# A hybrid attention and mixture-of-experts layer: the ring of expert weights refills four couples' places instead of three

## The reference

```python
def per_sequence(args):
    hs, cs = args
    a = jnp.einsum('sd,edf->sef', hs, w_gate)      # w_gate, w_up: (32, 1024, 256)
    u = jnp.einsum('sd,edf->sef', hs, w_up)
    act = jax.nn.silu(a) * u * cs[..., None].astype(hs.dtype)
    return jnp.einsum('sef,efd->sd', act, w_down)  # w_down: (32, 256, 1024)
x = x + hierarchical_moe(...)
return rms_norm(x, norm_final_g)
```

## Time and profile before

| | |
|---|---|
| median of 3 runs | 372.0 us (370.66, 372.0, 376.49) |
| the profiled execution's own time | 372.67 us |
| its span, first to last instruction | 370.9 us |
| granted TensorE clock, mean | 0.96 of full speed |
| TensorE busy | 311.2 us (84%) |
| VectorE, ScalarE, GpSimd busy | 167.8, 117.9, 42.2 us |
| moved by the DMA engines | 121.68 MB, mean 328 GB/s |
| VectorE's first copy of the end (line 1387) | starts at 362.66 us |

### The profile page before, as it was taken

One profiled execution on the slowest core, in us unless ns is written; L12 is line 12 of the kernel. 1 busy time (PEld: TensorE's weight loads), 2 busy tenths in 40 slices (PEclk: granted clock), 3 DMA queues, 4 the chain that ended last, 5 costly groups with the idle time before them and its releaser, 6 DMA issues.

```text
span 370.9 us, 11439 instructions
## 1 busy us (share of the span) xinstructions
PE 311.2 (84%) x4700; PEld 240.6 (65%) x4701; DVE 167.8 (45%) x445; ACT 117.9 (32%) x275; POOL 42.2 (11%) x65
## 2 busy tenths in 40 slices
PE   1799999999999899549979897979998997586571
PEld 1699989799775445237767665657766765566350
DVE  2637354565164514874435444344444443231334
ACT  4736156463244215621212222222222221120222
POOL 1200001451404023820000000000000000000002
PEclk9999999999999999968999999999999999588996
DMA  8999892080839782985999969999999999999953
GB/s 253 360 386 387 289 418 122 2 341 11 330 139 422 203 350 97 338 342 217 413 421 414 415 264 418 421 412 422 416 414 421 412 424 420 412 423 414 417 232 113
DMA packets 31434, 121.68 MB, mean 328 GB/s; under 512 B 5432, under 2 KB 7760, under 8 KB 23216
## 3 DMA queue, kind: packets, MB, share of 16 engines
q1 hardware_dynamic: 31264, 121.15, 82.8%
q10 hardware_dynamic: 144, 0.15, 0.1%
HBM read 120.24 MB, written 1.05 MB: 327 GB/s over the span
## 4 chain that ended last, share of the span: by engine, by line
PE 60%; DMA 7%; issue 7%; DVE 7%; SPq 7%; ACT 5%; DVEq 5%; POOL 0%; POOLq 0%; ACTq 0%
PE bank L448 12%; PE bank L717 8%; PE bank L513 8%; PE bank L659 7%; DMA ring<-in_w_up_dram 6%; PE bank L442 6%; SPq L328 4%; PE bank L696 4%; PE bank L669 4%; SPq L335 2%; ACT yb L960 2%; PE bank L462 2%; DVEq L1369 2%; PE bank L706 2%; DVEq L1368 2%
## 5 line engine op out<-in xcount | busy, mean ns | idle before, releaser
L696 PEld LDWEIGHTS bank<-ring,hT 128*32 128x32 f32 x2176 | 64.9, 118 | 33.3 <-issue 32.0
L696 PE MATMUL bank<-ring,hT 128*32 128x128 f32 x2176 | 70.4, 291 | 18.3 <-DMA ring<-in_w_up_dram 9.0
L1364 DVE SCALAR_TENSOR_TENSOR yb<-bank,pp,yb 64x512 fp32r<-64x512 f32 x36 | 27.0, 749 | 45.2 <-ACT yb L960 44.6
L659 PE MATMUL bank<-pp,qk 128*128 128x64 bf16 x912 | 31.7, 197 | 11.5 <-DVE pp L1297 8.6
L1107 DVE TENSOR_TENSOR unit_lo<-ring,unit_hi 128x2048 fp32r<-128x2048 f32 (+1 forms) x12 | 26.3, 2205 | 32.1 <-ACT unit_hi L783 32.0
L659 PEld LDWEIGHTS bank<-pp,qk 128*128 128x128 bf16 x912 | 29.2, 100 | 16.3 <-DVE pp L1297 11.6
L960 ACT ACTIVATE yb<-bank,pp 64x512 fp32r<-64x512 f32 x36 | 24.6, 682 | 29.0 <-PE bank L717 28.5
L717 PE MATMUL bank<-ring,pp 128*32 128x512 f32 x272 | 32.7, 598 | 0.1
L1022 POOL TENSOR_TENSOR stats<-stats 128x1 f32<-128x1 f32 (+1 forms) x7 | 4.3, 620 | 228.9 <-DVE stats L1395 205.3
L513 PE MATMUL bank<-ring,qk 128*128 128x512 f32 x64 | 29.3, 598 | 0.0
L950 ACT ACTIVATE pp<-bank 128x128 f32<-128x128 f32 x18 | 5.0, 277 | 70.8 <-PE bank L696 70.8
(11 more groups left out here) (195 smaller groups left out, 439.7 us busy)
## 6 DMA issues: line engine op xcount, KB each, us to landing
ring<-in_w_gate_dram SPq DMA_DIRECT2D x30, 1024.0 KB, 12.6
ring<-in_w_up_dram SPq DMA_DIRECT2D x30, 1024.0 KB, 16.0
ring<-in_w_down_dram SPq DMA_DIRECT2D x30, 1024.0 KB, 15.8
ring<-in_w_in_dram SPq DMA_DIRECT2D x5, 2048.0 KB, 20.3
ring<-in_w_out_dram SPq DMA_DIRECT2D x1, 4096.0 KB, 12.9
ring<-in_w_in_dram SPq DMA_DIRECT2D x2, 1024.0 KB, 7.7
work<-in_x_dram SPq DMA_DIRECT2D x2, 512.0 KB, 4.6
spare<-in_w_gate_dram SPq DMA_DIRECT2D x1, 1024.0 KB, 15.9
```

The lines of the kernel that those rows point to most:

```text
L659: last = mm(p_hg[:, k * CP:(k + 1) * CP], hs[:, i, t, k, :], selb[:, t, :], start=(t == 0 and i == 0), stop=(t == NT - 1 and i == 2))
L696: last = mm(p_gu[b:b + CAP, w * P:(w + 1) * P], hg[:, k, CAP * e:CAP * (e + 1)], w_gu[at[e]][:, w, k, h, :], start=(k == 0), stop=(k == KD ...
L1364: V.scalar_tensor_tensor(out=yb[half][rest, :], in0=p_y[rows, :], scalar=wcol[rows, :], in1=yb[half][rows, :].bitcast(fp32), op0=ALU.mult, ...
```

## The change

The ring goes round all four couples' places: places 6 and 7 are refilled too, and couple q from 4 on goes into the places of couple q - 4. TensorE's loop has four bodies and goes three times round; SyncE's loop over refills likewise has four and goes twice round, behind four refills written out. The last norm's weights no longer lie in `work`, which now holds the weights of couple 15, but in the head of the ring's place 0, which couple 12 used last; SyncE waits for couple 12's gate products before it issues them. The transfers themselves, their order and their sizes stay.

```diff
-TURN = 3
+RINGED = 6
+TURN = 4
-FIRST = TURN + 1
-LOOPS = (COUPLES - FIRST) // TURN
+LOOPS = COUPLES // TURN - 1
...
-        ring = sb("ring", [P, 2 * TURN * EXPERT])
+        ring = sb("ring", [P, RINGED * EXPERT])
...
-        gfin = work[:, 0:D]
+        gfin = ring[:, 0:D]
...
         def places(q):
-            if q == TURN:
-                return EXTRA, EXTRA + 1
-            s = q if q < TURN else (q - FIRST) % TURN
-            return 2 * s, 2 * s + 1
+            return 2 * (q % TURN), 2 * (q % TURN) + 1
...
             for q in range(TURN):
-                refill(q, [(2 * (q + FIRST) + i, places(q + FIRST)[i]) for i in range(2)])
+                refill(q, [(2 * (q + TURN) + i, places(q)[i]) for i in range(2)])
             with sp.Fori(1, LOOPS) as g:
                 for j in range(TURN):
-                    refill(g * TURN + (FIRST - TURN + j), [(2 * (g * TURN + (FIRST + j)) + i, places(FIRST + j)[i]) for i in range(2)])
+                    refill(g * TURN + j, [(2 * (g * TURN + (TURN + j)) + i, places(j)[i]) for i in range(2)])
+
+            sp.wait_ge(gate_done, sp.value_load(base[0:1, COUPLES - TURN + 1:COUPLES - TURN + 2], min_val=1, max_val=ITEMS_MAX))
             sp.dma_start(gfin, I["norm_final_g"].rearrange("(o d) -> o d", o=1).to_broadcast([P, D])).then_inc(gfin_in, 16)
...
             for q in range(TURN):
                 couple(q, places(q), (1, 1))
-            couple(TURN, places(TURN), (1, 1))
             with pe.Fori(0, LOOPS) as g:
                 for j in range(TURN):
-                    couple(g * TURN + (FIRST + j), places(FIRST + j), (g + 2, g + 2))
+                    couple(g * TURN + (TURN + j), places(j), (g + 2, g + 2))
```

More of the change, by code:

```diff
@@ L49 @@
 PASSES_MAX = SEQ // CAP
-TURN = 3
+RINGED = 6
+TURN = 4
 EXPERT = 3 * KD * FE
-FIRST = TURN + 1
-LOOPS = (COUPLES - FIRST) // TURN
-assert FIRST + LOOPS * TURN == COUPLES
+LOOPS = COUPLES // TURN - 1
+assert (LOOPS + 1) * TURN == COUPLES
 ITEMS_MAX = COUPLES * PASSES_MAX
@@ L216, in layer_program @@
         wcol = pp[:, M0 + 960:M0 + 961]
-        place = [ring[:, s * EXPERT:(s + 1) * EXPERT] for s in range(2 * TURN)] + [work[:, :]]
-        EXTRA = 2 * TURN
+        place = [ring[:, s * EXPERT:(s + 1) * EXPERT] for s in range(RINGED)] + [work[:, :]]
         gu_at = [s[:, 0:2 * KD * FE] for s in place] + [spare[:, :]]
@@ L245, in layer_program @@
         blk_in = [sem(f"blk_in{b}") for b in range(6)]
-        gate_in = [sem(f"gate_in{p}") for p in range(EXTRA + 2)]
-        up_in = [sem(f"up_in{p}") for p in range(EXTRA + 2)]
-        dn_in = [sem(f"dn_in{p}") for p in range(EXTRA + 2)]
+        gate_in = [sem(f"gate_in{p}") for p in range(2 * TURN)]
+        up_in = [sem(f"up_in{p}") for p in range(2 * TURN)]
+        dn_in = [sem(f"dn_in{p}") for p in range(2 * TURN)]
         out_done = sem("out_done")
@@ L339, in load @@
                 load_dn(e, e)
-            load_gu(2 * TURN + 1, EXTRA + 1)
+            load_gu(RINGED + 1, RINGED + 1)
             sp.wait_ge(w_lo_ready, 10)
@@ L368, in _ @@
             sp.wait_ge(logits_done, NT)
-            load_half(2 * TURN, EXTRA, 1)
+            load_half(RINGED, RINGED, 1)
             sp.wait_ge(acc_set, 1)
-            load_dn(2 * TURN, EXTRA)
+            load_dn(RINGED, RINGED)
             sp.wait_ge(r1_ready, 3)
-            load_half(2 * TURN, EXTRA, 0)
+            load_half(RINGED, RINGED, 0)
             sp.wait_ge(split_ready, 2)
-            load_dn(2 * TURN + 1, EXTRA + 1)
+            load_dn(RINGED + 1, RINGED + 1)
             sp.wait_ge(base_ready, 1)
```

## The result

The kernel after takes 370.99 us (median of 17 runs, 369.94 to 372.22) against 374.04 us for the kernel before on the same chip (17 runs, 370.66 to 376.49). The ratio is 0.9934, with a 95% interval of 0.9914 to 0.9955: faster by 2.5 us, between 1.7 and 3.2. (Ratios leave out the runs that count as slow, here three of before's, at 376.32 to 376.49 us; the medians shown are of all runs, and so the two medians lie 3.05 us apart.) The forecast was 368.7 against the 372.0 of the three runs shown, a ratio of 0.9911, or 3.35 us. The direction holds, and so does the mechanism of the hole; the gain is three quarters of the forecast, which lies just outside the interval.

The account below looks back on a forecast made before the run. The prediction took the landing of the last up halves, at the end of the transfer stream, as the bound. Closing the hole gives 372.0 - 3.35 = 368.65, say 368.7 us, all other parts 0; range 366.6 to 371.8.

Parts of the forecast that it names:

- The hole's worth: Thin transfers from 216 to 221 us, 138 against 417 GB/s: closing them was to gain 3.35 us.
- The tail behind the last up halves: From the landing of the last w_up to the span's end: to stay 18.0 us.
- The bound: The end is set by when the last up halves land: stream start, bytes at 417 GB/s, and any hole.
- Part 1: Couple 7's weights wait for couple 3, not couple 4, and are issued at about 208, not 218.73; the hole closes.
- Rival B: The lagging third of the DMA engines sets the end, so only 2.1 us is gained: 369.9 us; chance 0.12.
- Rival D: Without the hole the 16 engines drift apart and the slowest delays the end: 372.4 to 376.4 us; chance 0.07.
- Parts 2 and 3: Refills four couples ahead open no new hole, least margin 8 us; SyncE held earlier by a full queue costs 0 us.
- Part 4: The last norm's weights, issued last with an added wait on couple 12's gate products, cost 0 us.
- Part 5: TensorE's eighth couple body may add stalls of 1.5 us each, covered by its DMA waits: 0 us.
- Part 6: Couples 7, 11 and 15 read from work, spare and pp, with products taking the same 0.27 us each.
- Rival A: TensorE's last burst falls in the slow clock and costs 1.4 to 1.7 us: 370.1 to 370.6 us; chance 0.22.
- The chances: Odds for the measured verdict, with 2% as about what tells from no change: faster 0.02, same 0.95, slower 0.03.

Follow-up runs that it names:

- hole_back: The kernel after, but couple 7's weights wait for couple 4's products instead of couple 3's; median 374.78 us, 1.001 of the kernel before.
- late_rest: The kernel after, but refills from couple 8's on wait one couple longer, couple 7's does not; median 371.71 us, 0.994 of the kernel before.
- after_third: The kernel after, unchanged, run a third time; median 371.21 us, 0.994 of the kernel before.
- before_again: The kernel before, unchanged, run once more; median 373.44 us, ratio 1.000.
- before_third: The kernel before, unchanged, profiled a third time; one run of 372.33 us.
- late_all: The kernel after, but every refill from couple 7's on waits for the next couple's products; median 374.71 us, 0.999 of the kernel before.

## Why the prediction was right or wrong

Two terms of the sum failed, both in size. The hole's worth was put at 3.35 us, by the mean of the engines, and measured 2.6 us, because the end waits for the last engine. The tail behind the last up halves was left at 18.0 us, and in the kernel after it is 19.4 to 19.5 us, because its last burst falls in the slow clock. The rest of the account held.

**The bound.** Right: the end is set by the last up halves and a fixed tail. Holes of 1.9, 3.4 and 15.6 us moved the landing by 1.6, 2.6 and 14.8 us.

**Part 1, the hole and what closes it.** Right in place, cause and width. It was forecast that couple 7's refill is issued at about 208 (206.89) and that the slices between are full (419 GB/s). `hole_back` shows that this one refill is all of it.

**Its worth, the term that was mis-sized.** For the mean of the engines the reading was right (a hole of 3.4 us moved it by 3.3), and the end does not go by the mean. I weighed two readings and took the mean because the lagging third ran on by the same 1.3 to 1.5 us after 46 and after 138 us of stream. What I read as a lag that does not grow was a lag that had been set back at the hole and built up again by the code loads behind it. Without the hole the last drain takes 3.2 us. Measured worth in the stream: 2.6 us. Rival B gave 2.1 for a related reason (the laggards' own idle time), and its sign nearly came: with the first refill of before, 169.76, the landing of after is at 350.6, where B said 350.8 and I said 349.6. Rival D named the mechanism, that the hole is where the engines come together, and its sign came, a last drain of over 3 us. D was wrong in what drives the engines apart, which is the code loads and not the length of the stream, and in size: it needed a lag of 4.9 us to turn the sign. Its page of the Trainium skill (DMA: Bandwidth & Descriptors, "Two DMAs through the same engine are not ordered") says that nothing orders transfers across the 16 engines; the drains here agree, with 3.2 us against 1.8 between the first and the last engine.

**Parts 2 and 3, the margins and the full queue.** Right: no hole from couple 8 on, and the rate with a full queue is the same 416 to 417 GB/s. Even margins one couple shorter hold but for 0.2 us (late_rest). What I left out is the margin of couple 6, ahead of the change and untouched by it, which is the smallest of all and is missed in some executions.

**Part 4, the last norm's weights.** Right at 0 us: issued at 333.52, long after couple 12's gate products, and landed 22.8 us later, at 356.3, 5 us before VectorE's first copy of the end (361.28). **Part 5, the code.** No stall of TensorE shows at the end, as forecast; what one can do where no cover is, after_third shows. What the part left out is that code comes through the DMA engines of the stream: 12 loads of 16 KB in after, 11 in before, from 171 us on. **Part 6.** Right at 0.

**Rival A, the slow clock.** I gave it 0.22 and took the clock as before for the likeliest. All four profiles of this stream without extra products have it, at 1.5 us in all, within the price of 1.4 to 2.0, though split another way: the burst takes 2.5 to 3.3 us and the gather 1.8 to 2.5, up to 1.0 more than the 1.5 of before. Of the five profiles with the hole of 3.1 to 3.9 us and no extra products, four have a full clock in the last burst and a tail of 18.0 us (before, before_again, before_third, hole_back); late_all has 20.5. I argued that the median of before may hold such draws; the profiles say that it holds few. By the rule of the Trainium skill, TensorE: Matmul & The Clock Gate, "HAM oscillation — how this bites in real kernels", each burst behind a wait for data starts slow. The last bursts of the four profiles of after agree and those of before do not, nor does the burst of couple 14 in the profile of after, which took 1.95 us at 335.09 behind a wait of 3.03 us. Why the same wait of 3.0 us ends so differently in the two is open; that couple 15 now lies in work and spare is not it, since in hole_back it does too. Were both terms whole, 2.6 - 1.5 = 1.1 us would be left of the gain, and the runs show 2.5. Where the difference lies is not shown. It is likely in the slower runs of before: its profiled executions took 372.33, 372.67 and 373.76 us, and none of its runs above those was profiled.

**The chances.** Within 2% was right, and the time is in the range; the median that it was counted from, 372.0 of three runs, was 2 us below that of 17.

## What to carry to other kernels

Where a stream of transfers sets the end, look for the slices in which it is thin, and find the one trigger that comes too late; a ring that is longer everywhere is worth only what it is worth at that trigger. Price a hole by the last of the engines that share a stream, not by their mean: the drain at the end shows how far they are apart, and a hole in the middle may have hidden it. Look also for code loads on the same engines; here each put one engine behind, and only a gap in the stream cleared that. Then list the margins of all triggers, also of those that the change does not touch, since the next hole opens at the smallest.

## What the runs showed of the hardware that was not expected

Code loads of 16 KB run on the same 16 DMA engines as the data. Each took 1.0 to 1.1 us of one engine, and in after each was followed by that engine's share of every later transfer landing some 1.5 us later against the others; 12 of them spread the last up half over 3.6 us. With no code load, from 257 to 350 us at 417 GB/s, the spread did not change. A gap of 1.2 us near the end brought it down to 1.0 us, with the data no later than without the gap. And a few products with no use ahead of a 3.0 us wait went with a granted clock of 1.00 in the burst behind it in all three profiles of after that had them (1.96 us or less for 64 products against 2.5 to 3.3 us in the four without); three products of 0.5 us each were enough in the one profile that tried so few.
